# Issuing the read-back of the experts' moved rows when the last pair's slot weights are stored

## The chip, the core and the metric

The kernel runs on one core of one Trainium2 chip. The metric is the device time of one execution in microseconds (us). The core has TensorE (PE; its weight loads are shown apart as PEld), VectorE (DVE), ScalarE (ACT), GpSimd (POOL) and SyncE (SP), and 16 DMA engines that all queues share. In the profile, queue q1 carries what SP issues (the weights) and queue q0 what GpSimd issues.

## What is computed

A first transformer block (a retention layer, a latent-attention layer, two gated feed-forwards) over 16 + 256 tokens of width 1024 feeds a second block with a token mixer and a mixture of experts. Only the end of the second block matters here. 256 tokens each choose one of 4 groups and 2 of its 8 experts:

```python
def hier_moe(h, w_rg, b_rg, w_re, b_re, w_e_gate, w_e_up, w_e_down):
    t = h.reshape(-1, D)
    pg = jax.nn.softmax((t @ w_rg + b_rg).astype(jnp.float32), axis=-1)
    p_top, g_top = lax.top_k(pg, 1)
    ...
    v2, e2 = lax.top_k(le_g, TOPK_IN_GROUP)
    w2 = jax.nn.softmax(v2, axis=-1) * p_top
    ...
    for gi in range(N_GROUPS):
        a = jax.nn.silu(jnp.einsum('td,edf->tef', t, w_e_gate[gi])) * jnp.einsum('td,edf->tef', t, w_e_up[gi])
        y = y + jnp.einsum('tef,te,efd->td', a, comb[:, gi], w_e_down[gi])
    return y.reshape(B, S, D)

x = x + g2 * hier_moe(h, ...)
return rms_norm(x, final_norm_w)
```

All values are float32. The weights of the 32 experts are 3 x 1024 x 256 numbers each.

## The kernel before

The whole kernel is one stream of weight units of 512 KB (128 rows of 1024 floats), loaded by SP in the order in which TensorE uses them. The experts come last, in 16 pairs (`PAIRS`), numbered 0 to 15 here, of two experts each. A pair takes 12 units (`PAIR_UNITS`): 8 for gate and up, 4 for down. Even pairs use the 12 slots of `ring` (issued on L675); odd pairs use 12 other slots (issued on L703), of which units 0 to 3 lie in `tab`, 4 to 7 in `w_late` and 8 to 11 in `arena`. So gate and up of an odd pair need `tab` and then `w_late`, and its down product needs `arena`; TensorE waits for four such units at once. SP may refill a slot when TensorE has begun the unit after it (`unit_begun`), so weights run up to two pairs ahead of TensorE.

In one pair TensorE turns the selection and sums the weights of the pair's 2 x 64 token slots (L1472, L1474), multiplies gate and up (L1509), transposes the activation (L1541) and multiplies down (L1509). VectorE stores the slots' weights (`slot_w`, L2798, two reductions), and the second of these raises the semaphore `slot_w_stored`; it reaches 16 with pair 15.

The pairs' results go two ways. Pairs 0 to 11 (`MOVED` = 12) are *moved*: GpSimd writes their rows by an indirect DMA into the DRAM tensor `expert_rows` (L783), at two rows a token, one for each of its two experts. Pairs 12 to 15 are *scattered*: TensorE adds them into PSUM banks 4 to 7 by a matmul with the turned selection (L1487, L1488). At the end GpSimd reads `expert_rows` back, in two DMAs of 1 MB into the buffers `hn` and `sq` (L790). VectorE waits for both (`rows_read`), adds the two (L2871), TensorE turns the sum and adds it to the banks (L1580), and then come the last sum (L2878), the final norm (L902, L1633, L2121, L2126) and the stores.

Before, GpSimd issues the read-back as soon as all rows of pairs 0 to 11 have landed in DRAM (L787), while pairs 12 to 15 still run and their weights are still being loaded.

Of the kernel before, what the change touches and what calls it, by code (L numbers as in the profile page):

```python
# [60 lines left out]
PAIRS = NE // 2  # L61
# [197 lines left out]
def build(nc, weights, mod_rows, c_rows, vectors_in, tables_in, tokens_in, rel_bias, skew, expert_rows, out):  # L259
    with ExitStack() as ctx:  # L260
# [3 lines left out]
        def sem(name):  # L264
            return ctx.enter_context(nc.semaphore(name))
# [59 lines left out]

        o_r, o_lo = place(0, 4 * RH, T0)
        _, o_hi = place(4 * RH * T0, 4 * RH, T0)
        qk = carve(4, T0, at=8 * RH * T0)
        rope_t = carve(4, T0)
# [20 lines left out]
        ckv_at = 2 * DT * T0  # L350
        ckv, ckv_lo = place(ckv_at, KVT, T0)
        _, ckv_hi = place(ckv_at + KVT * T0, KVT, T0)
        hn_flat = hn[:, :, :].rearrange("p a b -> p (a b)")
        pt_at, meta_at = 2 * MLA_W, 2 * MLA_W + 6 * P
# [3 lines left out]
        cq_at = ckv_at + 2 * KVT * T0  # L358
        cq, cq_lo = place(cq_at, QT, SEQ)
        _, cq_hi = place(cq_at + QT * SEQ, QT, SEQ)  # L360
        krope = carve(1, T0, at=cq_at + 2 * QT * SEQ)
        k_m = carve(MH, T0)
# [95 lines left out]
        def flat2(a):  # L458
            return a.rearrange("p a b -> p (a b)")
# [45 lines left out]
        def S(name):  # L505
            if name not in made:
                made[name] = sem(name)
            return made[name]
# [236 lines left out]
        @block.gpsimd  # L745
        def _(pool):

            nc.gpsimd.memset(pool_pad, 0.0)
            nc.gpsimd.memset(mod_part[:, :, :], 0.0).then_inc(S("rel_zeroed"), 1)
            nc.gpsimd.memset(relb[:, :], NEG).then_inc(S("rel_zeroed"), 1)  # L750
            pool.wait_ge(S("rel_zeroed"), 2)
            pool.dma_start(relb[0:BUCKETS, :], rel_bias).then_inc(rel_loaded, 16)

            pool.wait_ge(S("bias_row"), 1)
            pool.dma_start(skew, bias_w.unsqueeze(1).to_broadcast([AH, P, 512])).then_inc(S("skew_written"), 16)
            for n in range(4):
                pool.dma_start(expert_rows[n * P:(n + 1) * P, :], flat2(mod_part)).then_inc(rows_moved[n % 2], 16)
            pool.dma_start(c_row, c_rows).then_inc(rel_loaded, 16)
            pool.wait_ge(rows_moved[0], 32)
            pool.wait_ge(rows_moved[1], 32)  # L760
            pool.dma_start(mod_row, mod_rows[0:P, :]).then_inc(mod_loaded, 16)
            pool.wait_ge(S("skew_written"), 16)
            pool.wait_ge(S("decayed"), RH)
            pool.wait_ge(S("roped"), 2 * RH)
            flat = P * 512
            for a in range(AH):
                for off, lo, n in ((255, 0, P), (127, P, SEQ)):
                    pool.dma_start(bias_a[:, a, lo:lo + n],
                                   bass.AP(skew.tensor, a * flat + off, [[511, P], [1, n]])).then_inc(S("bias_loaded"), 16)
            for n in range(1, MOD_TILES):  # L770
                pool.wait_ge(mod_used, n)
                pool.dma_start(mod_row, mod_rows[n * P:(n + 1) * P, :]).then_inc(mod_loaded, 16)  # L772
            pool.wait_ge(S("bias_loaded"), 16 * 2 * AH)

            pool.wait_ge(S("rounds_ready"), 1)
            pool_rounds = pool.value_load(rounds_t[0:1, 0:1], min_val=1, max_val=SEQ // CAP)
            with pool.Fori(0, pool_rounds) as r:
                with pool.Fori(0, MOVED // 2) as two:
                    for n in range(2):
                        pool.wait_ge(S("slot_w_stored"), r * PAIRS + two * 2 + (n + 1))  # L780
                        pool.wait_ge(S("out_hi_ready"), r * (2 * PAIRS) + two * 4 + (2 * n + 2))
                        pool.wait_ge(S("out_split"), r * (2 * PAIRS) + two * 4 + (2 * n + 4))
                        pool.indirect_dma_start(expert_rows, bass.IndirectOffsetOnAxis(ap=row_of[n][:, :], axis=0),  # L783
                                                out_row[n], None, bounds_check=r + (2 * SEQ - 1 + n),
                                                oob_is_err=False).then_inc(rows_moved[n], 16)
            for n in range(2):
                pool.wait_ge(rows_moved[n], pool_rounds * (8 * MOVED) + 32)  # L787
            nc.gpsimd.tensor_tensor(pool_pad[:, 1:2], pool_pad[:, 0:1], pool_pad[:, 0:1], ALU.mult)
            for n in range(2):
                pool.dma_start(sums_by_choice[n], expert_rows[n * SEQ:(n + 1) * SEQ, :].rearrange(  # L790
                    "(t p) d -> p t d", p=P)).then_inc(S("rows_read"), 16)
# [2117 lines left out]
```

## Time and profile before

| | us |
|---|---|
| median of 3 runs | 1345.79 |
| lowest, highest | 1344.12, 1351.33 |
| the profiled execution, its own time | 1348.65 |
| its span, from the first to the last instruction | 1346.8 |
| TensorE busy | 1298.9 (96% of the span) |
| VectorE, ScalarE, GpSimd busy | 808.1, 612.3, 48.6 |

All times of the trace are us from the start of the span; 1.85 us of the execution lie outside it. The rows shown further down come from the profile's page, from tables of stretches (busy time of each engine, the clock granted to TensorE as a share of full speed, DMA share and GB/s), from lists of instructions in order of time (start, length, engine, line, what is written and read, and in brackets the idle time before it with what ended it), from the chain of work that ended last, and from the view of DMA queues. An issue's time to landing runs from the issuing instruction to its last completion.

### The profile page before, as it was taken

The numbers are of one execution on the slowest core, as the hardware profiler recorded it, in microseconds if no ns is written. First come the engines' busy times: TensorE is split into PE (matmuls) and PEld (weight loads), VectorE is DVE, ScalarE is ACT, GpSimd is POOL, SyncE is SP. The second block draws the span as 40 slices with busy tenths as digits, with TensorE's granted clock in tenths as the row PEclk, the third lists the DMA queues.
The fourth block names the chain that finished last, engine by engine and source line by source line (L and its number), as shares of the span: only waits on it lengthen the run. The fifth ranks groups of instructions, "written<-read, shape, count | busy, mean of one in ns | idle before, by whom it ended". The sixth has DMA issues, their size and how long they took to land. (4 is left out here: it accounts for less than half of the span.)

```text
span 1346.8 us, 24698 instructions
## 1 busy us (share of the span) xinstructions
PE 1298.9 (96%) x9416; PEld 1130.7 (84%) x9416; DVE 808.1 (60%) x1461; ACT 612.3 (45%) x1047; POOL 48.6 (4%) x85
## 2 busy tenths in 40 slices
PE   6999999999999998999999999999999989999897
PEld 5999999999999998789999989989999954444344
DVE  6476557588766667467888757858645742222214
ACT  4545545544444544555544446656534441211112
POOL 0100020000000000000000000000000000000100
PEclk8999999999999999999999999999989999999999
DMA  9774355566667553235667776432123599999992
GB/s 372 171 247 161 126 175 179 178 219 220 219 220 242 196 184 129 79 109 188 234 229 232 256 245 215 157 109 79 64 94 125 172 396 369 416 418 418 418 419 104
DMA packets 83286, 295.77 MB, mean 220 GB/s; under 512 B 11062, under 2 KB 12086, under 8 KB 83056
## 3 DMA queue, kind: packets, MB, share of 16 engines
q1 hardware_dynamic: 72720, 263.68, 54.1%
q0 software_dynamic: 10464, 30.66, 7.8%
q8 instruction: 73, 1.20, 0.3%
q14 instruction: 29, 0.24, 0.1%
HBM read 287.76 MB, written 11.53 MB: 222 GB/s over the span
## 5 line engine op out<-in xcount | busy, mean ns | idle before, releaser
L2087 DVE TENSOR_TENSOR ring_low<-ring,w_hi 128x1024 fp32r<-128x1024 f32 x292 | 355.2, 1223 | 191.0 <-ACT w_hi L1605 190.3
L816 PE MATMUL bank<-hn_hi,w_hi 128*128 128x272 f32 (+1 forms) x1416 | 413.1, 292 | 4.4 <-DVE hn_low L2108 3.9
L820 PE MATMUL bank<-hn_hi,ring_low 128*128 128x272 f32 (+1 forms) x1416 | 406.6, 287 | 0.0
L819 PE MATMUL bank<-hn_low,w_hi 128*128 128x272 f32 (+1 forms) x1416 | 405.8, 287 | 0.0
L1605 ACT ACTIVATE w_hi<-ring 128x1024 fp32r<-128x1024 f32 x292 | 302.4, 1051 | 114.2 <-PE bank L816 105.9
L816 PEld LDWEIGHTS bank<-hn_hi,w_hi 128*128 128x128 f32 x1416 | 269.7, 190 | 8.2 <-DVE hn_low L2108 4.4
L819 PEld LDWEIGHTS bank<-hn_low,w_hi 128*128 128x128 f32 x1416 | 269.8, 191 | 0.3
L820 PEld LDWEIGHTS bank<-hn_hi,ring_low 128*128 128x128 f32 x1416 | 270.0, 191 | 0.0
L816 PE MATMUL bank<-arena_r,w_hi 128*128 128x256 f32 (+1 forms) x816 | 234.8, 288 | 4.5 <-DVE ring_low L2087 2.1
L820 PE MATMUL bank<-arena_r,ring_low 128*128 128x256 f32 (+1 forms) x816 | 232.9, 285 | 0.0
L819 PE MATMUL bank<-arena_r,w_hi 128*128 128x256 f32 (+1 forms) x816 | 232.4, 285 | 0.0
L816 PEld LDWEIGHTS bank<-arena_r,w_hi 128*128 128x128 f32 x816 | 154.7, 190 | 7.9 <-issue 4.6
L819 PEld LDWEIGHTS bank<-arena_r,w_hi 128*128 128x128 f32 x816 | 155.0, 190 | 0.1
L820 PEld LDWEIGHTS bank<-arena_r,ring_low 128*128 128x128 f32 x816 | 154.5, 189 | 0.0
L1509 PE MATMUL bank<-ring,arena 128*64 128x512 f32 x384 | 85.9, 596 | 2.7 <-ACT arena L2039 1.6
L1509 PEld LDWEIGHTS bank<-ring,arena 128*64 128x64 f32 x384 | 27.7, 137 | 48.8 <-issue 47.9
L2807 DVE TENSOR_TENSOR arena<-arena,bank 128x256 f32<-128x256 f32 x16 | 6.7, 421 | 100.8 <-ACT arena L2028 100.8
L2028 ACT ACTIVATE arena<-bank 128x256 f32<-128x256 f32 x16 | 6.1, 384 | 133.9 <-PE bank L1509 133.9
L2154 DVE CUSTOM_DVE_ANT_0 mod_part<-mod_part,arena,vec 128x1024 f32<-128x1024 f32 x40 | 51.2, 1279 | 9.0 <-DMA mod_part<-mod_rows 9.0
L1733 ACT ACTIVATE arena<-arena 128x272 f32<-128x272 f32 (+1 forms) x44 | 18.7, 425 | 74.1 <-DVE arena L2299 74.1
L772 POOL DMA_DIRECT2D mod_part<-mod_rows x39 | 20.6, 529 | 573.9 <-DVE mod L2154 573.9
L1509 PE MATMUL bank<-tab,arena 128*64 128x512 f32 x128 | 31.4, 637 | 5.3 <-DMA tab<-weights 5.3
(458 smaller groups left out, 1590.1 us busy)
## 6 DMA issues: line engine op xcount, KB each, us to landing
ring<-weights SPq DMA_DIRECT2D x396, 512.0 KB, 3.5
mod_part<-mod_rows POOLq DMA_DIRECT2D x40, 512.0 KB, 4.7
tab<-weights SPq DMA_DIRECT2D x32, 512.0 KB
arena<-weights SPq DMA_DIRECT2D x29, 512.0 KB, 14.5
w_late<-weights SPq DMA_DIRECT2D x28, 512.0 KB
tab<-tables SPq DMA_DIRECT2D x1, 2858.0 KB, 17.5
skew<-arena POOLq DMA_DIRECT2D x1, 2048.0 KB, 46.7
expert_rows<-mod_part POOLq DMA_DIRECT2D x4, 512.0 KB, 31.3
```

The costliest lines, as they stand in the source:

```text
L772: pool.dma_start(mod_row, mod_rows[n * P:(n + 1) * P, :]).then_inc(mod_loaded, 16)
L816: begun = mm(dst[:, 0:cols], wh, high(k), start=k == 0, stop=False)
L819: mm(dst[:, 0:cols], wh, low(k), start=False, stop=False)
L820: last = mm(dst[:, 0:cols], wl, high(k), start=False, stop=k == K - 1)
L1509: last = mm(dst[e * CAP:(e + 1) * CAP, :], x(e), unit[:, e * 512:(e + 1) * 512], start=start, stop=stop)
L1605: fn(w_hi[:, n % SPLITS, :], ring[:, u % SLOTS, :], ACT.Copy).then_inc(S("w_hi_ready"), 1)
L1733: fn(x, x, ACT.Silu).then_inc(S("ff_silu"), 1)
L2028: fn(flat2(e_gate), bank[2][:, 0:EF], ACT.Silu).then_inc(S("e_gate_ready"), 1)
L2087: tt_(ring_lo[:, slot, :], ring[:, slot, :], w_hi[:, n % SPLITS, :], ALU.subtract).then_inc(S("w_lo_ready"), 1)
L2154: nc.vector.tensor_tensor_reduce(mod_row, mod_row, c_row, 1.0, V("b_mod", n), ALU.mult, ALU.add, mod[:, n:n + 1]).then_inc(mod_used, 1)
L2807: tt_(flat2(e_act), flat2(e_gate), bank[2][:, EF:2 * EF], ALU.mult).then_inc(S("e_act_ready"), 1)
```

## The change

GpSimd gets one more wait between its wait for the moved rows and the read-back: it also waits until `slot_w_stored` shows that every pair of every round has stored its slots' weights, with pair 15 the last. Nothing else differs.

```diff
             for n in range(2):
                 pool.wait_ge(rows_moved[n], pool_rounds * (8 * MOVED) + 32)
+            pool.wait_ge(S("slot_w_stored"), pool_rounds * PAIRS)
             nc.gpsimd.tensor_tensor(pool_pad[:, 1:2], pool_pad[:, 0:1], pool_pad[:, 0:1], ALU.mult)
             for n in range(2):
                 pool.dma_start(sums_by_choice[n], expert_rows[n * SEQ:(n + 1) * SEQ, :].rearrange(
```

GpSimd's queue after its loop over the moved pairs, before (lines one lower) and after; `rows_moved0` and `rows_moved1` count the landed rows of even and odd pairs:

```order
L787 ISA
L788 ISA
L788 TENSOR_TENSOR pool_pad<-pool_pad 128x1 [waits rows_moved1,rows_moved0]
L790 DMA hn<-expert_rows 128x2x1024
L790 DMA sq<-expert_rows 128x2x1024
```

```order
L787 ISA
L788 REGISTER_ALU [waits rows_moved1,rows_moved0]
L789 ISA
L789 TENSOR_TENSOR pool_pad<-pool_pad 128x1 [waits slot_w_stored]
L791 DMA hn<-expert_rows 128x2x1024
L791 DMA sq<-expert_rows 128x2x1024
```

The two DMAs and the small product ahead of them now stand behind `slot_w_stored`. The other four engines have the same rows as before.

## Rows read from the trace of the kernel before

**Rows 1.** The page, part 2: 40 slices of the span, tenths of full clock, of DMA.

```profile
PEclk8999999999999999999999999999989999999999
DMA  9774355566667553235667776432123599999992
```

**Rows 2.** PE and PEld in order of time, where weights ended a wait.

```profile
1250.86 1.51 PE L1509 MATMUL bank<-w_late,arena 128*64 128x512 f32 x6 [0.18 <-DMA w_late<-weights]
...
1280.30 5.85 PE L1509 MATMUL bank<-tab,arena 128*64 128x512 f32 x16 [5.31 <-DMA tab<-weights]
1287.11 3.65 PE L1509 MATMUL bank<-w_late,arena 128*64 128x512 f32 x16 [0.96 <-DMA w_late<-weights]
...
1317.11 0.14 PEld L1509 LDWEIGHTS bank<-w_late,arena 128*64 128x64 f32 x2 [0.35 <-DMA w_late<-weights]
```

**Rows 3.** Chain of work that ended last, between 1260 and 1291 us.

```profile
1267.44 19.62 DMA w_late<-weights
...
1287.11 3.65 PE bank L1509 x16
```

**Rows 4.** Table by stretch: us, busy of each engine, PEclk, DMA share, GB/s.

```profile
1250.86:1287.11 36.25, 29.68 (x141) 12.82 (x141) 6.90 (x21) 5.51 (x14) 2.65 (x4) 0.91 1.03 418
1287.11:1317.11 30.00, 28.83 (x156) 13.92 (x157) 6.93 (x21) 5.96 (x14) 0.00 (x0) 1.00 1.02 417
...
1277.00:1278.00 1.00, 0.00 (x0) 0.00 (x0) 0.00 (x0) 0.00 (x0) 0.00 (x0) 0.97 1.06 434
1278.00:1279.00 1.00, 0.00 (x0) 0.00 (x0) 0.00 (x0) 0.00 (x0) 0.00 (x0) 0.50 1.01 414
1284.00:1285.00 1.00, 1.00 (x4) 0.21 (x3) 0.00 (x0) 0.00 (x0) 0.00 (x0) 0.62 1.02 418
1285.00:1286.00 1.00, 1.00 (x6) 0.14 (x2) 0.00 (x0) 0.00 (x0) 0.00 (x0) 1.00 1.03 422
```

**Rows 5.** POOL in order of time, 1269 to 1272 us.

```profile
1269.41 0.19 POOL L788 TENSOR_TENSOR pool_pad<-pool_pad 128x1 f32<-128x1 f32 x1 [6.09 <-DMA expert_rows<-arena,row_of]
1269.87 0.77 POOL L790 DMA_DIRECT2D hn<-expert_rows  x1 [0.27 <-issue]
1270.64 0.73 POOL L790 DMA_DIRECT2D sq<-expert_rows  x1
```

**Rows 6.** DMA queues, 1273 to 1286 us: packets, MB, share of 16 engines; issues.

```profile
q1 hardware_dynamic: 907, 3.31, 62.5%
q0 software_dynamic: 544, 2.10, 39.5%
...
ring<-weights SPq DMA_DIRECT2D x7, 512.0 KB, 17.4
```

**Rows 7.** DMA queue q0 alone, from 1273 to 1280.3 us.

```profile
q0 software_dynamic: 358, 1.40, 47.1%
```

**Rows 8.** DMA queue q0 alone, 1251 to 1256 us (one moved pair's rows).

```profile
q0 software_dynamic: 144, 0.15, 8.6%
```

**Rows 9.** DVE and PE in order of time, pair 15 and the end.

```profile
1315.10 0.33 DVE L2798 TENSOR_REDUCE arena<-bank 64x1 f32<-64x2 f32 x2
...
1329.66 2.35 DVE L2871 TENSOR_TENSOR hn<-hn,sq 128x1024 f32<-128x1024 f32 x2
...
1324.55 3.65 PE L1509 MATMUL bank<-arena 128*64 128x512 f32 x16 [0.47 <-ACT arena L2039]
```

**Rows 10.** DMA queues, 1321 to 1322 us, then all packets of 1322 to 1325.

```profile
q1 hardware_dynamic: 15, 0.05, 11.5%
...
DMA packets 0, 0.00 MB, mean 0 GB/s; under 512 B 0, under 2 KB 0, under 8 KB 0
```

**Rows 11.** DMA queues, 1273.5 to 1274 us, the read-back's first packets.

```profile
q1 hardware_dynamic: 40, 0.15, 75.0%
q0 software_dynamic: 12, 0.05, 23.9%
```

**Rows 12.** DMA queues, 1274 to 1282 us.

```profile
q0 software_dynamic: 434, 1.71, 52.4%
q1 hardware_dynamic: 438, 1.60, 49.0%
```

**Rows 13.** DMA issues of GpSimd over the span: KB each, median us to landing.

```profile
mod_part<-mod_rows POOLq DMA_DIRECT2D x40, 512.0 KB, 4.7
...
expert_rows<-mod_part POOLq DMA_DIRECT2D x4, 512.0 KB, 31.3
...
hn<-expert_rows POOLq DMA_DIRECT2D x1, 1024.0 KB, 10.6
sq<-expert_rows POOLq DMA_DIRECT2D x1, 1024.0 KB, 14.8
```

## The prediction

> **What bounds the kernel now.** I began with the page's slices [rows 1]. Over most of the span the 16 DMA engines are partly idle, but the last eighth stands at 9 tenths: there the experts' weights come as fast as DMA can bring them. In the same place the clock granted to TensorE dips once. The list of TensorE's work shows why [rows 2]: nearly all its waits for weights lie between 1250.86 and 1317.11 us, above all 5.31 us ahead of pair 13's first gate units (`tab`) and 0.96 us ahead of its later ones (`w_late`). Two more are so small (0.18 us at 1250.86; at 1317.11 a weight load idle for 0.35 us) that they say something else: TensorE and the stream of weights arrive together there, with no reserve. The chain of work that ended last agrees [rows 3]: for 19.62 us it runs through the loading of `w_late`, and then through TensorE.
>
> So here the end is set by the weights, and the question about any other byte on the DMA engines is whether it lies ahead of these weights. The table by stretch prices it [rows 4]. From 1250.86 to 1287.11 and from 1287.11 to 1317.11 the same thing happens, 24 units are brought, at 418 and 417 GB/s and a DMA share above 1.0. The first takes 36.25 us and the second 30.00 us. What is extra in the first is GpSimd's traffic: two moved pairs' rows and the read-back.
>
> **What the change removes.** The read-back is issued at 1269.87 and 1270.64 us [rows 5]. Its 2.10 MB pass in 1273 to 1286 us and take 39.5% of the 16 engines over 13 us, which is 5.14 us of all of them [rows 6]; by bytes it is 2.10 MB / 418 GB/s = 5.02 us. A third way: 36.25 - 30.00 = 6.25 us, less two moved pairs' rows at 8.6% of 5 us = 0.43 us each [rows 4, 8], leaves 5.39 us. The three bound the term between 5.0 and 5.4; I take 5.1, the value between the two that measure the read-back itself. All of it is over before `w_late` of pair 13 lands at 1287.11, and since these engines are saturated before and after, everything behind it in the stream comes 5.1 us earlier: `w_late` of pair 13 at 1282.0, that of pair 15 at 1312.0.
>
> **What TensorE makes of it.** It is ready for pair 13's `tab` at 1280.30 - 5.31 = 1275.0 us. By 1280.3 the read-back had taken 47.1% of 7.3 us = 3.4 us [rows 7], so `tab` now lands near 1276.9, and TensorE waits 1.9 us in place of 5.31. Its 16 products took 5.85 us, against 3.65 us for the same form just behind [rows 2], because the granted clock had fallen to 0.50 (1.2 GHz) during the wait and was back at 1.00 only by 1285 [rows 4]. With a wait of 1.9 us I expect it to stay at 1.00: they end by 1276.9 + 3.65 = 1280.6, and TensorE waits 1.4 us more for `w_late`, which it starts at 1282.0. From there to 1317.11 it had hardly waited for a weight. So its own work of 30.0 us brings it to 1312.0, the very time at which pair 15's `w_late` lands. That second meeting is why the gain is not more than 5.1 us, though 6.27 us of waits and 2.2 us of slow clock stand in the rows: the stream itself only gains what was taken out of it.
>
> SP issues weights as slots come free, and slots come free as TensorE begins units. Both run 5.1 us earlier, and a ring unit issued in this stretch lands a median of 17.4 us after its issue [rows 6]: the backlog waits in the DMA queue, and SP is not what limits it.
>
> **What the change adds.** One wait on GpSimd. Behind it in its queue are only the small product and the two read-back DMAs, and behind these VectorE's sum on L2871, TensorE's L1580 and the final norm. The semaphore was raised at 1315.10 + 0.33 = 1315.43 us [rows 9], now 1310.3. From the start of the small product to the first issue are 0.46 us [rows 5], so the issues stand at about 1310.9 and 1311.7. The rows are wanted on L2871, at 1329.66 before [rows 9] and 1324.6 after the shift, 12.9 us after the second issue. How long will it take? The nearest row on the long side is the same DMA in the saturated stretch, 10.6 and 14.8 us; on the short side, 4.7 us for half as much in an easy stretch [rows 13]. The weights' stream thins out at once behind the issue, as its last packets ran at 1321 to 1322 us before [rows 10], now 1316.9. I reckon 3.6 us to the first packet, as before (1269.87 to 1273.5 [rows 5, 11]), 5.1 us of its own, up to 2.4 us shared on the engines that still carry weights, and 1 us to the completion: 1323.0 us. That leaves 1.6 us. It costs nothing, and at the worst end (14.8 us) 1311.7 + 14.8 = 1326.5, 1.9 us late.
>
> It can also hurt the last weights, the `arena` units of pair 15's down product, on the slowest DMA engines. Half of an engine goes to each queue while both have work (52.4% and 49.0% [rows 12]). With first packets at 1310.9 + 3.6 = 1314.5, the slowest engine has 2.4 us of weights left and finishes them at 1319.3. They are wanted at 1324.55 - 5.1 = 1319.4 [rows 9]. That is a margin of 0.1 us, and the weakest step of the sum. Were the first packets to come without any delay, the weights would be done at most 5.1 us late, at 1322.0, and TensorE would lose 2.6 us. So this term lies between 0 and 2.6; I take 0, since on just those engines the read-back finds a queue as full as it found at 1269.87.
>
> **Two rules against rows.** A read-back issued at 1269.87 is wanted 60 us later, and it displaced weights that were wanted at once [rows 5, 6, 9]. The Trainium skill, page "DMA: Bandwidth & Descriptors", section "Rules for kernel authors", says to issue a DMA early, compute, and wait for it late, because its fixed cost is then hidden. By that rule the old place is the better one and the change gains nothing or loses the read-back's latency; the trace speaks against it here, because the engines are full. The first packets came 3.6 us after the issue [rows 5, 11]. The same page, section "Latency and other measured facts", puts the first byte of a DMA issued by GpSimd at about 1 us. By that figure, as an estimate, the packets would start at 1311.9, and the last weights would be 2.5 us late, which is the first rival below; the row decides for 3.6 us.
>
> **The sum.** On the profiled execution: 1348.65 - 5.1 + 0 = 1343.55 us. It ran 2.86 us above the median of the three runs, so against the median: 1345.79 - 5.1 = 1340.7 us.
>
> **The rivals.**
> *A, the late read-back and the last weights collide.* Packets start sooner than 3.6 us, or the rows land late. For it: a margin of 0.1 us, and engines that have finished their weights are free to start at once. Against it: only the slowest engines count. Price 0 to 2.6 us, say 1.3: 1342.0 us.
> *B, the clock still falls.* If the waits of 1.9 and 1.4 us bring 0.50 again, `tab`'s products end at 1276.9 + 5.85 = 1282.8, 0.8 us behind `w_late`, and the next block can lose 2.2 us more. Gain 2.1 to 4.3: 1342.6 us. Against it: TensorE was idle from 1275.0, and the clock stood at 0.97 over 1277 to 1278, so it fell only near 1278 [rows 4]; both waits would be shorter than that.
> *C, more is gained than the bytes.* If in other executions the stream has a little reserve at 1317.11, the whole of 6.27 + 2.2 = 8.5 us can go: 1337.3 us. Against it: the two meetings in rows 2.
> *D, the stream isn't the limit, or the wait does nothing.* If the wait is met at once or the stream was paced by SP, nothing changes: 1345.8 us. Against it: the semaphore's last step stands at 1315.43, and DMA shares above 1.0.
> *E, slower: the read-back lands far too late.* Its place is VectorE's wait ahead of L2871. The four DMAs that clear these rows early in the kernel took a median of 31.3 us to land [rows 13]. Would the read-back take as long, its second half would land at 1311.7 + 31.3 = 1343.0, against 1324.6: +18.4 - 5.1 = 13.3 us slower, 1359.1 us. It turns the gain into a loss once the landing takes over 12.9 + 5.1 = 18 us. Against it: those were writes to DRAM that shared the engines with the first weights, and the read-back itself took 14.8 us at most beside full load.
>
> **How the numbers follow.** Chances: forecast 53%, A 23%, B 6%, C 8%, D 6%, E 4%. The forecast's own range is 1339 to 1343. A measurement of this kernel can tell about 0.5%, 6.7 us, from no change; the forecast's 5.1 us is 0.38%. The three runs of before spread over 7.2 us, so a median can stand 2 us off. The range goes from C (1337.3) to the near side of D, 1337.5 to 1345.0; outside lie E, most of D and a part of C. Faster by over 0.5% (below 1339.1) are C and the forecast's low edge: 16%. Slower by over 0.5% is E: 4%. The remaining 80% are within 0.5%.
>
> **What would show it.** In the trace after: L791 issued behind pair 15's L2798, near 1311; queue q0 empty between 1273 and 1286; `tab` of pair 13 awaited for about 2 us in place of 5.31 and its products at full clock; `w_late` of pair 13 begun near 1282.0 and of pair 15 near 1312.0; pair 15's down product not waiting for DMA (A shows there); L2871 directly behind L2819 (E and half of A show there); span near 1341.7. I am wrong if the stretch between the two `w_late` landings of pairs 11 and 13 is still near 36 us, or if a new wait stands behind 1312.

## The result and the profile after

| | us |
|---|---|
| before, median of 10 runs | 1345.8 (1344.12 to 1351.33) |
| after, median of 10 runs | 1342.84 (1341.37 to 1346.94) |
| ratio after to before | 0.9976, 95% interval 0.9965 to 0.9987 |
| the profiled execution of after, its own time and span | 1342.55, 1340.8 |

The change makes the kernel 3.2 us faster (0.24%) by this ratio, whose interval reaches from 1.7 to 4.7 us. Two later comparisons of the same two kernels, on record below, gave 0.9961 and 0.9958, that is 5.2 and 5.7 us. The forecast was 5.1 us.

TensorE's waits for weights, in the list in order of time of the kernel after (start, length, engine, line, what is written and read; idle time before and what ended it). Its lines are one higher than those of before. They answer to [rows 2]:

```profile
1249.74 3.65 PE L1510 MATMUL bank<-w_late,arena 128*64 128x512 f32 x16
...
1276.09 3.65 PE L1510 MATMUL bank<-tab,arena 128*64 128x512 f32 x16 [2.21 <-DMA tab<-weights]
1281.03 3.65 PE L1510 MATMUL bank<-w_late,arena 128*64 128x512 f32 x16 [1.29 <-DMA w_late<-weights]
...
1311.02 0.14 PEld L1510 LDWEIGHTS bank<-w_late,arena 128*64 128x64 f32 x2 [0.32 <-DMA w_late<-weights]
...
1311.41 3.60 PE L1510 MATMUL bank<-w_late,arena 128*64 128x512 f32 x16
```

The wait of 5.31 us for pair 13's `tab` is 2.21 us, and the 16 products behind it take 3.65 us in place of 5.85. `w_late` of pair 13 is begun at 1281.03 and that of pair 15 at 1311.41. The same two stretches as in [rows 4], from the table by stretch (busy time of PE, PEld, DVE, ACT, POOL; granted clock, DMA share, GB/s):

```profile
1249.74:1281.03 31.29, 27.50 (x140) 12.29 (x140) 6.90 (x21) 5.52 (x14) 0.96 (x1) 1.00 1.03 418
1281.03:1311.41 30.38, 29.20 (x157) 14.06 (x159) 7.08 (x21) 5.96 (x14) 1.64 (x3) 1.00 1.02 415
```

The first is 31.29 us instead of 36.25: 4.96 us less at the same 418 GB/s. The clock stands at 1.00 (2.4 GHz) over it, where it had dipped to 0.50. DMA queues of after from 1273 to 1286 us, against [rows 6]:

```profile
q1 hardware_dynamic: 1484, 5.41, 102.2%
...
ring<-weights SPq DMA_DIRECT2D x11, 512.0 KB, 14.8
```

Queue q0 has no row left there; q1 moves 5.41 MB where it moved 3.31. Ring units land 14.8 us after their issue, not 17.4. The read-back now stands at the end. GpSimd in order of time, then the issues with their time to landing, and what queue q0 and q1 moved in 1317 to 1318 us:

```profile
1309.45 0.20 POOL L789 TENSOR_TENSOR pool_pad<-pool_pad 128x1 f32<-128x1 f32 x1 [47.26 <-DVE arena L2799]
1309.59 0.77 POOL L791 DMA_DIRECT2D hn<-expert_rows  x1
1310.36 0.74 POOL L791 DMA_DIRECT2D sq<-expert_rows  x1
```

```profile
hn<-expert_rows POOLq DMA_DIRECT2D x1, 1024.0 KB, 8.0
sq<-expert_rows POOLq DMA_DIRECT2D x1, 1024.0 KB, 10.6
```

```profile
q0 software_dynamic: 69, 0.22, 54.5%
q1 hardware_dynamic: 9, 0.02, 5.2%
```

The second half lands at 1310.36 + 10.6 = 1321.0. Who waits at the end, TensorE's last down product and VectorE's sum:

```profile
1318.48 3.65 PE L1510 MATMUL bank<-arena 128*64 128x512 f32 x16 [0.47 <-ACT arena L2040]
```

```profile
1322.93 0.75 DVE L2820 SCALAR_TENSOR_TENSOR arena_r<-bank,arena,arena_r 128x512 fp32r<-128x512 f32 x1 [0.96 <-ACT arena_r L2050]
1323.60 2.35 DVE L2872 TENSOR_TENSOR hn<-hn,sq 128x1024 f32<-128x1024 f32 x2
```

The down product follows ScalarE after 0.47 us, as it did before [rows 9], and not a DMA, though q1 still moves a last 0.02 MB in 1317 to 1318 us. The sum stands directly behind the work ahead of it; the rows have been there for 2.6 us. Nothing new is waited for.

### The profile page after: what moved, and what is told of

Read it like the earlier page. It is cut to its first block and busy times, and to the rows that moved or that the text cites. A ratio compares the mean times of both kernels' runs of the same rounds, so it can differ in the third digit from the quotient of the medians.

```text
span 1340.8 us, 24699 instructions
## 1 busy us (share of the span) xinstructions
PE 1297.0 (97%) x9416; PEld 1130.5 (84%) x9416; DVE 808.4 (60%) x1461; ACT 612.8 (46%) x1047; POOL 48.7 (4%) x85
## 5 line engine op out<-in xcount | busy, mean ns | idle before, releaser
L1726 ACT ACTIVATE arena_r<-arena 128x272 fp32r<-128x272 f32 (+1 forms) x44 | 18.5, 421 | 39.5 <-DVE arena L2308 39.5
```

What stands on the lines that cost most here:

```text
L1726: fn(ff_hi[:, pair, 0:cols], ff_gate[:, pair % 2, 0:cols], ACT.Copy).then_inc(S("ff_hi_ready"), 1)
```

## The experiments

Two theories. **S**: the end follows the stream of weights, and the read-back costs its 5.0 us wherever it stands ahead of pair 15's last gate and up weights. **R**: a usual execution has about 2 us in reserve, the first profile had none, so only some 3 us reach the end. All ran beside the kernel before, in three groups, each on one chip: the first four, the next four, the last two.

### The kernel before again

No edit.

> The kernel before, unchanged, to get a second profile of it and the noise of a ratio. Theory S (the stream of weights): every execution loses the read-back's 5.0 us between the two w_late landings; then this profile again shows about 36.2 us from pair 11's w_late to pair 13's, and a time near 1346. Theory R (reserve): the first profile (1348.65 us, 2.86 above its median) caught an execution in which TensorE and the stream met without reserve, and in a usual one the stream is ahead by some 2 us, so that of the 5.0 us only about 3 reach the end; then the waits on DMA in this profile sum to about 2 us less than the 6.3 us of the first. Ratio to before 1.000 by both, within 0.001.

Measured: ratio 0.9998 [0.9985, 1.0012]; the profiled execution took 1347.43 us, a span of 1345.6. TensorE in order of time:

```profile
1249.62 3.65 PE L1509 MATMUL bank<-w_late,arena 128*64 128x512 f32 x16 [0.20 <-DMA w_late<-weights]
...
1278.78 5.01 PE L1509 MATMUL bank<-tab,arena 128*64 128x512 f32 x16 [5.02 <-DMA tab<-weights]
1285.90 3.65 PE L1509 MATMUL bank<-w_late,arena 128*64 128x512 f32 x16 [2.12 <-DMA w_late<-weights]
```

1285.90 - 1249.62 = 36.28 us, against 36.25 in the first profile, and the two waits sum to 7.1 us, where the first had 6.3 and R wanted some 4. R falls on this profile, whose execution lies 0.5 us above the median of its group.

### The kernel after again

No edit.

> The changed kernel again, on the same chip as its companions. Theory S: 5 us under before, ratio 0.9963. Theory R: 3 us under before, ratio 0.9977, with less than the 3.5 us of waits on DMA that its first profile showed, or an end set by TensorE's own work.

Measured: 0.9961 [0.9948, 0.9973]. In its profile `tab` is awaited for 2.24 us and `w_late` for 1.29 us, as in the first. This is what theory S expects.

### No read-back at all

```diff
-            for n in range(2):
-                pool.dma_start(sums_by_choice[n], expert_rows[n * SEQ:(n + 1) * SEQ, :].rearrange(
-                    "(t p) d -> p t d", p=P)).then_inc(S("rows_read"), 16)
...
-            dve.wait_ge(S("rows_read"), 32)
```

> The changed kernel with neither of the two read-back DMAs and without VectorE's wait for them; the sum adds what lies in the two buffers, so the moved rows are missing from the output. It prices the read-back as a whole. If the late read-back is fully hidden: the same time as the changed kernel, within 0.7 us. If it still costs (rival A: it collides with the last down weights, or lands late): faster than the changed kernel by up to 2.6 us. Against before: theory S 5 us (0.9963), theory R 3 us (0.9978) if hidden.

The output of this kernel lacks the moved rows. Measured: 0.9967 [0.9956, 0.9979], beside 0.9961 for the changed kernel on the same chip: no gain over it. TensorE in order of time:

```profile
1275.65 3.65 PE L1507 MATMUL bank<-tab,arena 128*64 128x512 f32 x16 [2.16 <-DMA tab<-weights]
```

The waits are those of the changed kernel (2.16 us here). The late read-back is hidden, to about 0.1 us by the profiles (table below), and rival A is out. There is nothing left to win by moving it.

### The wait one pair earlier

```diff
-            pool.wait_ge(S("slot_w_stored"), pool_rounds * PAIRS)
+            pool.wait_ge(S("slot_w_stored"), pool_rounds * (PAIRS - 1))
```

> The changed kernel with the new wait one pair earlier: the read-back is issued when pair 14's slot weights are stored, near 1295 us, so its 2.1 MB pass in about 1298 to 1309 us, still ahead of pair 15's gate and up weights but behind all of pair 13's. If what counts is bytes ahead of the last weights that TensorE waits for (theory S), the gain at pair 13 is given back at pair 15: no waits of 5 us at 1275, but one of about 5 us at 1306 to 1312, and the time of before, 1345 to 1346. If what counts was the stall at pair 13 with its fall of the clock: near the changed kernel, 1342 to 1343. If there is a reserve of about 2 us at pair 15 (theory R): between, about 3 us above the changed kernel.

Measured: 1.0007 [0.9996, 1.0018], no better than before. TensorE in order of time, then the sum:

```profile
1274.83 3.65 PE L1510 MATMUL bank<-tab,arena 128*64 128x512 f32 x16 [2.22 <-DMA tab<-weights]
1279.77 3.65 PE L1510 MATMUL bank<-w_late,arena 128*64 128x512 f32 x16 [1.28 <-DMA w_late<-weights]
1309.95 5.35 PE L1510 MATMUL bank<-tab,arena 128*64 128x512 f32 x16 [3.25 <-DMA tab<-weights]
```

```profile
1327.32 2.35 DVE L2872 TENSOR_TENSOR hn<-hn,sq 128x1024 f32<-128x1024 f32 x2
```

The stall at pair 13 is cut just as in the changed kernel, and a new one of 3.25 us stands at pair 15's `tab`. The products behind it take 5.35 us, again in part at half the clock. This is the run that says what the place has to be: behind the last awaited weights, not merely later.

### Half of it at each place

```diff
-        pool_pad = sb("pool_pad", P, 2)[:, :]
+        pool_pad = sb("pool_pad", P, 4)[:, :]
...
-            pool.wait_ge(S("slot_w_stored"), pool_rounds * PAIRS)
             nc.gpsimd.tensor_tensor(pool_pad[:, 1:2], pool_pad[:, 0:1], pool_pad[:, 0:1], ALU.mult)
             for n in range(2):
+                if n:
+                    pool.wait_ge(S("slot_w_stored"), pool_rounds * PAIRS)
+                    nc.gpsimd.tensor_tensor(pool_pad[:, 2:3], pool_pad[:, 0:1], pool_pad[:, 0:1], ALU.mult)
                 pool.dma_start(sums_by_choice[n], expert_rows[n * SEQ:(n + 1) * SEQ, :].rearrange(
```

> The first MB of the read-back (into hn) is issued at the old place, behind pair 11's rows, and only the second (into sq) behind pair 15's slot weights. Theory S (each byte ahead of pair 15's w_late costs its time at 418 GB/s): one MB costs 2.5 us, so the time lies half way, 2.5 us under before and 2.5 us above the changed kernel, ratio 0.998. Rival (the stall at pair 13 is lost in steps, by a fall of the clock or a queue that is either blocked or not): nearly all or nearly none of the 5 us.

Measured: 0.9984 [0.9972, 0.9995], 2.2 us under before (0.7 to 3.8): between the two kernels, near the half way that S expects. In its profile the clock fell too, and here it cost something. TensorE in order of time, then the stretch 1284 to 1286 us (granted clock 0.50):

```profile
1282.95 6.15 PE L1512 MATMUL bank<-tab,arena 128*64 128x512 f32 x16 [4.70 <-DMA tab<-weights]
...
1288.93 3.60 PE L1512 MATMUL bank<-w_late,arena 128*64 128x512 f32 x16
```

```profile
1284.00:1286.00 2.00, 2.00 (x8) 0.57 (x6) 0.00 (x0) 0.00 (x0) 0.00 (x0) 0.50 1.03 420
```

With 6.15 us for `tab`'s products TensorE comes to `w_late` without a wait: it is late itself, and this takes about 1 us off the gain (1.5 us by the table below, where 2.5 were due). So the profile does not show half of the 5 us but less, and the fall of the clock accounts for the rest.

### One MB more at the old place

```diff
+            late_read = hn_late_flat[:, 0:2 * D].rearrange("p (t d) -> p t d", t=2)
+            pool.dma_start(late_read, expert_rows[0:SEQ, :].rearrange("(t p) d -> p t d", p=P)).then_inc(S("rows_read"), 16)
             for n in range(2):
                 pool.dma_start(sums_by_choice[n], expert_rows[n * SEQ:(n + 1) * SEQ, :].rearrange(
...
-            dve.wait_ge(S("rows_read"), 32)
+            dve.wait_ge(S("rows_read"), 48)
```

> The kernel before with one MB more read back at the old place (the first half once more, into a buffer that nothing reads; VectorE waits for all three). Theory S: 2.5 us slower than before, ratio 1.0019. Rival (TensorE had waits in reserve that take up more traffic, or q0 is served beside q1 for nothing): no change.

Measured: 1.0044 [1.0027, 1.0061], 5.9 us slower (5.2 by the table below), not 2.5. The size expected was wrong, and the list of TensorE's work says why. Below it stands the stretch 1289 to 1291 us:

```profile
1249.98 3.65 PE L1511 MATMUL bank<-w_late,arena 128*64 128x512 f32 x16 [0.16 <-DMA w_late<-weights]
1279.41 5.88 PE L1511 MATMUL bank<-tab,arena 128*64 128x512 f32 x16 [5.28 <-DMA tab<-weights]
1288.75 6.33 PE L1511 MATMUL bank<-w_late,arena 128*64 128x512 f32 x16 [3.46 <-DMA w_late<-weights]
```

```profile
1289.00:1291.00 2.00, 2.00 (x6) 0.52 (x6) 0.00 (x0) 0.00 (x0) 0.00 (x0) 0.50 1.02 414
```

1288.75 - 1249.98 = 38.77 us: those are the 2.5 us for one MB, on top of 36.25. But the second wait is 3.46 us now, and the block behind it takes 6.33 us instead of 3.65: 2.7 us that nothing behind it takes up. This is a second fall of the clock (0.50 in the stretch), and it lies on the path that sets the end. In the kernel before the slow block had ended at 1286.15, ahead of the weights that came at 1287.11, and so was free.

### One MB more at the new place

The same edit on the changed kernel.

> The changed kernel with one MB more read back at the new place, ahead of the two halves (into a buffer that nothing reads; VectorE waits for all three). It asks how much slack the late read-back has. In the changed kernel it lands at 1321.0 and is wanted at 1323.6. One MB more is 2.5 us of all engines, plus 0.8 us of issue beside it: it lands at 1323.5 to 1324.3, so 0 to 0.7 us slower than the changed kernel, and still 4.3 to 5 us under before (ratio 0.9963 to 0.9968). Rival A (the last down weights are held up by it): the down product of pair 15 waits for DMA, 1 to 2.6 us.

Measured: 0.9961 [0.9944, 0.9978], the changed kernel's value. Three DMAs take 7.8, 9.5 and 12.2 us to land; the last is issued at 1312.73 and lands at 1324.9, and VectorE's sum stands at 1325.24, directly behind the work ahead of it. The last down product again follows ScalarE after 0.47 us. So the new place has room for at least 1 MB more, and rival A is out here too.

### Nine us later

```diff
             pool.wait_ge(S("slot_w_stored"), pool_rounds * PAIRS)
+            pool.wait_ge(S("act_t_stored"), pool_rounds * PAIRS)
```

> The changed kernel with one wait more: the read-back goes when ScalarE has stored pair 15's turned activation, at 1318.4 in place of 1309.4. It measures the cost of being late. Issued near 1318.9 and 1319.7 with the DMA engines idle, it needs 1.2 us to its first packet, 5.0 us of data and 1 us to complete: it lands near 1326.5 where it is wanted at 1323.6, so 2.9 us slower than the changed kernel (2 to 4.4), and 2 us under before, ratio 0.9985. If the landing is as slow as in the changed kernel (10.6 us from the second issue): 1330, so 6.7 us slower and 1.7 us slower than before.

Measured: 1.0010 [0.9997, 1.0023], against the 0.9961 of the run on the same chip with the issue at the new place (the one above, with 1 MB more): 6.6 us above it and not 2.9. TensorE's `tab` of pair 13, then VectorE and TensorE at the end, the two DMAs' times to landing, and the clock over 1330 to 1332:

```profile
1276.03 5.35 PE L1511 MATMUL bank<-tab,arena 128*64 128x512 f32 x16 [2.21 <-DMA tab<-weights]
```

```profile
1328.38 2.36 DVE L2873 TENSOR_TENSOR hn<-hn,sq 128x1024 f32<-128x1024 f32 x2 [4.59 <-DMA sq<-expert_rows]
```

```profile
1329.65 6.39 PE L1582 MATMUL bank<-tab,hn 128*128 128x128 f32 x32 [4.61 <-DVE hn L2873]
```

```profile
DMA to landing us min/median/max: 5.3/6.8/8.4
```

```profile
1330.00:1332.00 2.00, 2.00 (x11) 2.00 (x11) 0.74 (x1) 0.00 (x0) 0.00 (x0) 0.50 0.00 0
```

The rows land 8.4 us after the second issue at 1319.92, and the sum is 1328.38 - 1323.60 = 4.8 us late. Then TensorE, idle for 4.61 us, turns the sum at a clock of 0.50: 6.39 us, where the same 32 products took 3.84 us in the kernel before. That is the second part, 2.5 us. Rival E's mechanism is real, though far smaller than the 31.3 us that E had for a landing; at which delay short of nine us it begins was not tried.

### The kernel after a third time

No edit.

> The changed kernel once more, since its two comparisons so far gave 0.9976 [0.9965, 0.9987] and 0.9961 [0.9948, 0.9973]. Theory S: 0.9963 again, 5 us. Theory R (a part of the 5 us is lost in a share of the executions): nearer 0.997, 4 us. In the profile: about 31.3 us between the w_late landings of pairs 11 and 13, and either 3.65 us for the 16 products from pair 13's tab (clock at 1.00) or 5.35 us (clock fell during the wait of 2.2 us), which then costs 0.5 us.

Measured: 0.9958 [0.9943, 0.9972]. In this profile the clock fell, as rival B has it. TensorE, its weight loads, and the stretch 1281 to 1282 us:

```profile
1280.19 5.33 PE L1510 MATMUL bank<-tab,arena 128*64 128x512 f32 x16 [2.18 <-DMA tab<-weights]
1285.36 3.60 PE L1510 MATMUL bank<-w_late,arena 128*64 128x512 f32 x16
```

```profile
1285.10 0.40 PEld L1510 LDWEIGHTS bank<-w_late,arena 128*64 128x64 f32 x4 [0.46 <-DMA w_late<-weights]
```

```profile
1281.00:1282.00 1.00, 1.00 (x6) 0.28 (x4) 0.00 (x0) 0.00 (x0) 0.00 (x0) 0.50 1.02 418
```

The clock fell behind a wait of 2.18 us here, and did not behind 2.21 and 2.24 us in the two other profiles of this kernel. It fell in three of the five profiles whose read-back stands behind pair 15's slot weights: here, with 1 MB more at the new place (2.19 us) and nine us later (2.21 us). It stayed at 1.00 behind 2.16 us with no read-back and 2.22 us with the wait one pair earlier. So the length of the wait does not decide it. The price is small: the slow block takes up the 1.3 us that TensorE would have waited for `w_late` anyway, and `w_late` of pair 13 is begun 31.47 us after that of pair 11 (1285.36 - 1253.89), where 31.29 and 31.30 stood without the fall.

### No moved rows written

```diff
-                        pool.indirect_dma_start(expert_rows, bass.IndirectOffsetOnAxis(ap=row_of[n][:, :], axis=0),
-                                                out_row[n], None, bounds_check=r + (2 * SEQ - 1 + n),
-                                                oob_is_err=False).then_inc(rows_moved[n], 16)
...
-                    act.wait_ge(rows_moved[j % 2], moved * 16 + 32)
...
-                    dve.wait_ge(rows_moved[j % 2], moved * 16 + 32)
```

> The changed kernel without the twelve indirect writes of the moved rows to DRAM and without the waits on them; the read-back stays and brings what the tensor was cleared to, so the moved pairs are missing from the output. It asks what bounds the changed kernel now. Theory S: its remaining waits for weights at pair 13 (2.2 and 1.3 us) are still the stream's, which is 12 x 0.43 = 5.2 us shorter without these writes, so both waits go and TensorE's own work is the bound: 3.5 us under the changed kernel, 8.5 us under before, ratio 0.994. Rival (the waits come from SP's issue, which follows TensorE): the waits stay, same time as the changed kernel.

The moved pairs are missing from the output of this kernel. Measured: 0.9933 [0.9911, 0.9956], 9.0 us under before and 3.4 us under the changed kernel beside it (0.9958). TensorE's waits for weights are gone. What is left of them (who waited for whom, 1240 to 1330 us) are two weight loads of 0.3 us idle each, the usual gap between the loads of such a block. Below it, `w_late` of pairs 13 and 15:

```profile
PEld bank L1499 <- DMA w_late<-weights: 0.6, 2, 0.3
```

```profile
1273.79 3.60 PE L1499 MATMUL bank<-w_late,arena 128*64 128x512 f32 x16
...
1304.12 3.60 PE L1499 MATMUL bank<-w_late,arena 128*64 128x512 f32 x16
```

So the changed kernel is still held by the stream for about 3.5 us, and it goes free when the moved rows' traffic, too, is taken from ahead of the weights. The edit also drops the waits of ScalarE and VectorE on the landed rows; from 1225 us on, no such wait held either engine in the changed kernel.

### All profiles together

The executions differ most in when they come to pair 11's `w_late`, long before the change acts: from 1248.48 to 1254.13 us in these eleven profiles. (The run without moved rows is not among them, since its edit acts before that point.) Counted from there, executions of the same kernel hardly differ. Start of pair 11's `w_late`, start of VectorE's sum, and the execution's time less that start:

| kernel | pair 11's `w_late` | sum | sum less it | time less it |
|---|---|---|---|---|
| before | 1250.86 | 1329.66 | 78.80 | 97.79 |
| before, again | 1249.62 | 1328.47 | 78.85 | 97.81 |
| after | 1249.74 | 1323.60 | 73.86 | 92.81 |
| after, again | 1249.69 | 1323.58 | 73.89 | 92.85 |
| after, third | 1253.89 | 1327.88 | 73.99 | 92.96 |
| no read-back | 1249.34 | 1323.12 | 73.78 | 92.77 |
| one pair earlier | 1248.48 | 1327.32 | 78.84 | 97.84 |
| half each | 1254.13 | 1331.45 | 77.32 | 96.28 |
| 1 MB more, old place | 1249.98 | 1333.99 | 84.01 | 103.00 |
| 1 MB more, new place | 1251.22 | 1325.24 | 74.02 | 92.97 |
| nine us later | 1249.69 | 1328.38 | 78.69 | 100.21 |

From this point on the change is worth 4.8 to 5.0 us in every pair of profiles of the two kernels.

## Why the prediction was right, step by step

**What is removed.** 5.1 us, bounded by 5.0 and 5.4. Measured 36.25 - 31.29 = 4.96 us, and 4.94 us at VectorE's sum. The estimate by bytes, 5.02 us, was the best of the three. The one by difference, 5.39, took the two stretches of [rows 4] to hold the same weights, and they do not. DMA queues of before over the first and over the second stretch, then queue q0 of after over its first:

```profile
q1 hardware_dynamic: 3487, 12.70, 85.8%
q1 hardware_dynamic: 3428, 12.48, 101.9%
```

```profile
q0 software_dynamic: 288, 0.33, 2.9%
```

The first carries 0.22 MB more of weights, 0.5 us at 418 GB/s, which is the surplus. The moved rows were about right: 2.9% of 31.29 us = 0.91 us, against the 0.86 us taken off. No row of queue q0 is left between 1273 and 1286 us.

**What TensorE makes of it.** Waits of 1.9 and 1.4 us were forecast, 2.21 and 1.29 came. That the clock would stay at 1.00 came in the first profile, but that was luck: it fell in three of the five profiles with the read-back at the new place. `w_late` of pair 13 was to be begun at 1282.0 and that of pair 15 to land at 1312.0: 1281.03 and about 1311.0, each 1 us earlier, because this execution came 1.12 us earlier to pair 11. That there is no reserve at pair 15 is shown by the run with the wait one pair earlier: what is taken away at pair 13 and put back ahead of pair 15 is lost in full. But the prediction was wrong to give this second meeting as the reason why the gain is not more. From `w_late` of pair 13 to that of pair 15 TensorE takes 30.38 us after (1281.03 to 1311.41) and 30.33 us without moved rows (1273.79 to 1304.12), where it waits for no weights at all, so the meeting holds nothing up. The gain is set at pair 13's `w_late`, which comes 5.0 us earlier and is still awaited for 1.29 us.

**What is added.** The issues were to stand at 1310.9 and 1311.7, 1309.59 and 1310.36 came, the same less 1.3. The landing was to be at 1323.0, 1.6 us ahead of its use; it was 1321.0, 2.6 ahead. The weakest step, 0.1 us between the last weights and the down product, held for a reason other than mine. The first packets did not take 3.6 us: queue q0 already moves data in 1311 to 1312 us, below, so 1.4 to 2.4 us after the first issue. Queue q1 was down to 73.5% there, so some engines had time for it; that this is why the packets came sooner is argued, not shown. The last weights still came in time, in 1317 to 1318 us, where the prediction had 1319.3 and the down product that uses them began at 1318.48; the run without any read-back was not faster. DMA queues of after, 1311 to 1312 us:

```profile
q1 hardware_dynamic: 84, 0.30, 73.5%
q0 software_dynamic: 7, 0.03, 31.4%
```

The Trainium skill's figure of about 1 us to the first byte (page "DMA: Bandwidth & Descriptors", section "Latency and other measured facts") was nearer to this than my row, but the 2.5 us of delay that I had worked out with it did not come. The Trainium skill's rule to issue early and wait late (same page, section "Rules for kernel authors") is contradicted here by 0.9958 to 0.9976 for the later issue. The run with the issue nine us later shows what it guards against: 1.0010.

**The sum.** 1340.7 us was forecast and 1342.84 measured, 2.1 us more and inside the range. The mechanism has its 5.0 us in the profiles. The first comparison's 0.9976 [0.9965, 0.9987] just misses the 0.9963 that 5.0 us would be; the two others, 0.9961 and 0.9958, hold it. I put the 2 us to the spread of 5.6 us with which executions come to pair 11, where both kernels are the same; that this spread, and not a cause of its own, made the first comparison smaller is argued, not shown.

**The rivals.** A did not occur. B did, in three of five profiles, and so was far likelier than the 6% that I gave it. It cost 0.1 to 0.2 us by the table, in place of the 0.8 to 3.0 us that I had for it, since the slow block ended soon after `w_late` was due and the clock was back before the next block (3.60 us). C and D did not. E did not either; its wait appeared only in the run with the issue nine us later, and at 4.6 us.

## What to carry to other kernels

Where DMA engines are full and TensorE waits for what they bring, look for transfers that are wanted only at the end. Here 2.1 MB ahead of the last awaited weights cost 5.0 us, near their bytes at the stream's rate, and nothing behind them. Bytes alone give the time of the stream and not that of the kernel: the profiles have 3.5 us for 1 MB ahead of the weights, 5.0 for 2 and 10.2 for 3, because the slow clock behind a wait is sometimes hidden and sometimes not. It is not enough to move it later: one pair too early gave nothing, and nine us too late cost the whole gain and, by the profile, 2.4 us more. Gate it on an event of the last tile, and compare executions from the last point that they share before the change acts.

## What was not expected of the hardware

A wait of TensorE's is dearer than its length once the block behind it is on the path: 4.61 us of idleness at the end were followed by 32 products in 6.39 us in place of 3.84, and 3.46 us ahead of `w_late` by 6.33 us in place of 3.65. The same length of wait may or may not bring it: the clock went to 0.50 behind 2.18, 2.19 and 2.21 us and stayed at 1.00 behind 2.16, 2.21, 2.22 and 2.24. A DMA of GpSimd's put its first packet 3.6 us after the issue where the weights' queue was full on all engines, and 1.4 to 2.4 us where it had begun to thin out.
